# FFN norms in a diffusion backbone: 1/rms multiplied on behind the gate and up products, the shift as two extra columns

## The chip, the cores and the metric

One core of one Trainium2 chip runs the whole program. The metric is the device time of one execution in microseconds, as the median of several runs. The engines are TensorE (PE; its weight loads are shown as PEld), VectorE (DVE), ScalarE (ACT), GpSimd (POOL) and SyncE (SP), which issues most DMAs. They are tied together by semaphores only, and each works through its own instructions in the order written.

## The reference

Four layers. Each has a half-step SwiGLU FFN, a token mixer and a second half-step FFN, on 128 context tokens (xp) and 256 latent tokens (xs) of width 1024. Each sub-layer begins with an RMSNorm with adaLN modulation. The mixers are, in turn, gated DeltaNet, differential attention, a pooling mixer, and gated DeltaNet again. A final RMSNorm ends it.

```python
def _rms(x, g):
    y = xf * lax.rsqrt(jnp.mean(xf * xf, axis=-1, keepdims=True) + EPS) * g
def _adanorm(x, g, shift, scale):
    return _rms(x, g) * (1.0 + scale) + shift
def _half_ffn(x, m, j0, g, wg, wu, wd):
    h = _adanorm(x, g, m[:, :, j0], m[:, :, j0 + 1])
    f = (jax.nn.silu(h @ wg) * (h @ wu)) @ wd
    return x + 0.5 * m[:, :, j0 + 2] * f
...
for i in range(DEPTH):
    mp = _modulation(c_ctx[None, :], w_mod[i], b_mod[i])   # silu(c) @ w + b, 9 vectors of 1024
    ms = _modulation(c, w_mod[i], b_mod[i])
    xp = _half_ffn(xp, mp, 0, ...); xs = _half_ffn(xs, ms, 0, ...)
    # mixer on _adanorm(x, ..., 3, 4), with gate 5
    xp = _half_ffn(xp, mp, 6, ...); xs = _half_ffn(xs, ms, 6, ...)
```

Shift, scale and gate are vectors over channels, one set for context and one for latent tokens. D_FF is 2816.

## The kernel before

The residual stream `x` lies in SBUF as three token tiles of 128 tokens by 1024 channels. The program is a row of 12 stages, `r` = 0 to 11; stage r is an FFN when r % 3 is 0 or 2 and a mixer when it is 1. So there are 8 FFNs (stages 0, 2, 3, 5, 6, 8, 9, 11), and the crossings into them are: one at the start, four from a mixer (2, 5, 8, 11), three from an FFN (3, 6, 9). Four stages are entered as mixers from an FFN (1, 4, 7, 10).

Every product with weights is made of three float32r products. A value is rounded to its high part (`xT_hi`, `split_hi`, `hid_hi`, by ACT) and the difference is its low part (`xT_lo`, `split_lo`, `hid_lo`, by DVE); PE then adds hi x hi, hi x lo and lo x hi (`three`, line 1605).

**An FFN** works in 22 units. Unit j holds 128 columns of the gate weights, 128 of the up weights and 128 rows of the down weights: three parts of 128 x 1024, loaded by SP into two slots of `raw`. PE runs for each unit a gate pass (8 channel tiles x 3 matmuls of 384 token columns into bank 6), an up pass (the same into bank 7), and then the down pass of the unit before (3 token tiles x 2 halves x 3 matmuls of 512 columns into banks 0 to 5, which add up over the 22 units). ACT: rounds parts 0 and 1 of the next unit (line 778), takes silu of the gate bank (846), rounds the hidden tile (850), rounds part 2 of the next unit. DVE: `rest_part` 0 and 1 (the low parts, 1112), `hidden` = silu x up bank (1197), `hid_lo` (1199), `rest_part` 2, and then in the units that carry it the modulation work for the next layer, four `mod_junk` operations (398), each a product with a sum over a row of 1024. In FFNs 0 to 6 the 18 units of the middle bodies carry it (in FFN 0 also the first and the last two). SP loads the modulation weights and the raw parts in one order, and a modulation load waits for the DVE work before it.

**A crossing.** The residual (1225, 1228 on DVE, 622 on POOL): for each of three token tiles DVE multiplies two halves of the down banks by the gate (`gate_bc`) into three buffers `res_tmp`, POOL adds the first half to `x` and DVE the second. Then the norm: ACT squares a token tile with its row sum (809), POOL makes 1/rms (611, 612, a power of -0.5), DVE multiplies the tile by it into `xhat` (1158), PE transposes 24 blocks (1629), ACT applies scale and shift while it copies from PSUM (825, into four rows of `scratch`), and DVE casts to `xT_hi` (1172) and subtracts to `xT_lo` (1173). Each of the 8 channel tiles lets the first gate pass of the stage go on by three matmuls. In between PE makes the gate rows (1615): 4 matmuls of 512 columns that spread the gate vector of the stage over all partitions, which ACT copies to `gate_bc` (802). `diag`, their input, is made by DVE in the last body of the stage before (`gates`). In stage 0 the gate rows come behind the first up pass.

**Stage 0** begins with the modulation vectors themselves: five units on PE (2037), seven on DVE, all waiting for 1 MB loads; `normalised_rows(0)` stands in that work on DVE.

The order on each engine is written by hand; no scheduler moves anything.

## Time and profile before

| | us |
|---|---|
| median of 3 runs | 3479.87 |
| lowest, highest | 3478.95, 3481.42 |
| the profiled execution | 3476.7 |
| its span | 3474.9 |

The mean granted TensorE clock over the span is 0.973 of full. PE matmul is busy for 95% of the span, DVE for 68%, ACT for 38%, POOL for 9%. Busy time of PE is modelled, so its pace is better read from the starts of matmuls in the timeline. In the timeline a row has its start in us, its length in us, the engine, the line, the operation, out<-in, and in brackets how long the engine had been idle and what released it. Rows of the same kind that follow each other are merged (x4).

### The profile page before, as it was taken

To read this page: it belongs to the slowest core of one execution; us is meant where nothing else is said; L and a number is where in the kernel's file an instruction comes from. 1 tells how busy PE (TensorE), PEld (TensorE's weight loads), DVE (VectorE), ACT (ScalarE), POOL (GpSimd) and SP (SyncE) were. 2 spreads that over 40 slices of the span, in tenths; PEclk is the share of its full clock that TensorE was granted. 3 is DMA by queue.
4 is the path that set the end of the run, shared out by engine and by line. 5 is a ranking of instruction groups with operands and counts; after the bars stand their busy time and mean duration, and the time that the engine had idled before them with its cause. 6 is when DMAs were issued, how large, how long until landed. Compare 5 with 4: busy or idle time off the path is not lost.

```text
span 3474.9 us, 49765 instructions
## 1 busy us (share of the span) xinstructions
PE 3284.8 (95%) x18156; PEld 3051.1 (88%) x18156; DVE 2361.9 (68%) x3692; ACT 1310.5 (38%) x2253; POOL 297.2 (9%) x347
## 2 busy tenths in 40 slices
PE   7899999989999999879999998799999999999998
PEld 7799898979998998858998997699899988997997
DVE  7677876666776775566776777777767786666333
ACT  2233565243334334354334333333333366533332
POOL 0000104520000001000000001000000010540000
PEclk9999999999999999999999999899999999999999
DMA  6555220034544553213553553255345431013331
GB/s 261 208 211 211 101 81 1 25 134 181 211 183 162 208 202 121 85 49 140 211 214 131 200 206 153 79 211 211 146 192 205 189 107 57 14 49 109 127 127 73
DMA packets 62770, 502.77 MB, mean 145 GB/s; under 512 B 6416, under 2 KB 14608, under 8 KB 16448
## 3 DMA queue, kind: packets, MB, share of 16 engines
q1 hardware_dynamic: 60512, 493.12, 36.9%
q0 software_dynamic: 2144, 8.11, 0.6%
q8 instruction: 73, 1.20, 0.1%
q14 instruction: 41, 0.34, 0.0%
HBM read 496.49 MB, written 4.72 MB: 144 GB/s over the span
## 4 chain that ended last, share of the span: by engine, by line
PE 84%; DVE 9%; ACT 2%; issue 2%; DMA 1%; POOL 1%; SPq 0%; DVEq 0%; ACTq 0%; POOLq 0%
PE bank L1605 74%; PE bank L1768 7%; DVE xT_lo L1173 1%; DVE res_tmp L1225 1%; PE bank L1793 1%; DVE mod_junk L398 1%; DVE x L1228 1%; DMA mod_first<-mod_w 1%; DVE xT_hi L1172 1%; DVE split_lo L1112 1%; POOL rstd L612 1%; PE bank L1861 1%; PE bank L1719 1%; ACT split_hi L778 0%; DVE at_small L1489 0%
## 5 line engine op out<-in xcount | busy, mean ns | idle before, releaser
L1605 PE MATMUL bank<-xT_hi,split_hi 128*128 128x384 f32 (+1 forms) x3344 | 1142.5, 342 | 20.0 <-ACT silu_g L846 16.2
L1605 PE MATMUL bank<-xT_lo,split_hi 128*128 128x384 f32 (+1 forms) x3344 | 1132.3, 339 | 0.0
L1605 PE MATMUL bank<-xT_hi,split_lo 128*128 128x384 f32 (+1 forms) x3344 | 1131.6, 338 | 0.0
L1112 DVE TENSOR_TENSOR split_lo<-raw,split_hi 128x1024 fp32r<-128x1024 f32 x644 | 765.3, 1219 | 457.9 <-ACT split_hi L778 457.7
L778 ACT ACTIVATE split_hi<-raw 128x1024 fp32r<-128x1024 f32 x644 | 653.0, 1053 | 671.8 <-DMA raw<-ffn_w 367.8
L398 DVE SCALAR_TENSOR_TENSOR mod_junk<-mod_raw,cond 128x1024 f32<-128x1024 f32 x536 | 655.8, 1224 | 59.7 <-DVE mod_junk L398 33.3
L1605 PEld LDWEIGHTS bank<-xT_hi,split_hi 128*128 128x128 f32 (+1 forms) x3344 | 629.0, 188 | 43.0 <-DVE split_lo L1112 17.0
L1605 PEld LDWEIGHTS bank<-xT_lo,split_hi 128*128 128x128 f32 (+1 forms) x3344 | 629.0, 188 | 8.8 <-issue 0.4
L1605 PEld LDWEIGHTS bank<-xT_hi,split_lo 128*128 128x128 f32 (+1 forms) x3344 | 628.6, 188 | 1.1
L1605 PE MATMUL bank<-split_lo,hid_hi 128*128 128x512 f32 x1056 | 411.0, 389 | 0.0
L1605 PE MATMUL bank<-split_hi,hid_hi 128*128 128x512 f32 x1056 | 411.0, 389 | 0.0
L1605 PE MATMUL bank<-split_hi,hid_lo 128*128 128x512 f32 x1056 | 411.0, 389 | 0.0
L850 ACT ACTIVATE hid_hi<-hidden 128x384 fp32r<-128x384 f32 x176 | 92.4, 525 | 783.5 <-DVE hidden L1197 783.5
L622 POOL TENSOR_TENSOR x<-x,res_tmp 128x512 f32<-128x512 f32 x36 | 45.9, 1275 | 2479.2 <-DVE res_tmp L1225 2479.2
L1605 PEld LDWEIGHTS bank<-split_hi,hid_lo 128*128 128x128 f32 x1056 | 198.2, 188 | 41.1
L1605 PEld LDWEIGHTS bank<-split_hi,hid_hi 128*128 128x128 f32 x1056 | 198.1, 188 | 34.8
L1605 PEld LDWEIGHTS bank<-split_lo,hid_hi 128*128 128x128 f32 x1056 | 198.2, 188 | 34.7
L1197 DVE TENSOR_TENSOR hidden<-silu_g,bank 128x384 f32<-128x384 f32 x176 | 96.7, 549 | 162.2 <-PE bank L1605 162.2
L1199 DVE TENSOR_TENSOR hid_lo<-hidden,hid_hi 128x384 fp32r<-128x384 f32 x176 | 98.3, 558 | 109.0 <-ACT hid_hi L850 109.0
L1605 PE MATMUL bank<-split_hi,xT_hi 128*128 128x384 f32 (+2 forms) x360 | 136.4, 379 | 35.4 <-DVE xT_lo L1534 21.4
L1243 DVE SCALAR_TENSOR_TENSOR scratch<-scratch,cols 128x193 f32<-128x193 f32 x384 | 131.1, 415 | 12.0 <-ACT scratch L877 11.7
L1605 PE MATMUL bank<-split_lo,xT_hi 128*128 128x384 f32 (+2 forms) x360 | 133.2, 370 | 0.0
(247 smaller groups left out, 3068.2 us busy)
## 6 DMA issues: line engine op xcount, KB each, us to landing
raw<-ffn_w SPq DMA_DIRECT2D x176, 1536.0 KB, 7.6
mod_raw<-mod_w SPq DMA_DIRECT2D x134, 1024.0 KB, 4.8
raw<-a_in_w SPq DMA_DIRECT2D x20, 1536.0 KB, 6.3
raw<-b_in_w SPq DMA_DIRECT2D x8, 1536.0 KB, 6.3
raw<-a_out_w SPq DMA_DIRECT2D x4, 1536.0 KB, 7.7
mod_first<-mod_w SPq DMA_DIRECT2D x5, 1024.0 KB, 21.5
mod_first<-mod_rows SPq DMA_DIRECT2D x5, 1024.0 KB, 23.5
raw<-b_out_w SPq DMA_DIRECT2D x2, 1536.0 KB, 6.8
```

Of the source, the lines that this page charges most:

```text
L398: eng.scalar_tensor_tensor(mod_junk[:], weights[:, t], 1.0, cond[:, c], ALU.mult, ALU.mult, accum_out=mod_column(layer, unit, t, c)).then_ ...
L612: pool.tensor_tensor(rstd[:, span], rstd[:, span], neg_half[:, span], ALU.pow).then_inc(ready, 1)
L622: pool.tensor_tensor(x[:, t, 0:512], x[:, t, 0:512], res_tmp[:, 2 * t % 3], ALU.add).then_inc(res_pool, 1)
L778: act.activation(split_hi[:, unit.slot, q, 0:w], raw[:, unit.slot, q, 0:w], ACT.Copy).then_inc(hi_ready, 1)
L850: act.activation(hid_hi[:, par], hidden[:, par], ACT.Copy).then_inc(hid_hi_done, 1)
L1112: dve.tensor_tensor(split_lo[:, unit.slot, q, 0:w], raw[:, unit.slot, q, 0:w], f32(split_hi[:, unit.slot, q, 0:w]), ALU.subtract).then_inc ...
L1172: steps.settle(dve.tensor_copy(xT_hi[:, k], row))
L1197: dve.tensor_tensor(hidden[:, par], silu_g[:, par], ps[BANK_UP][:, 0:T], ALU.mult).then_inc(prod_done, 1)
L1199: dve.tensor_tensor(hid_lo[:, par], hidden[:, par], f32(hid_hi[:, par]), ALU.subtract).then_inc(hid_done, 1)
L1243: dve.scalar_tensor_tensor(dst, src, weight, dst, ALU.mult, ALU.add).then_inc(conv_step, 1)
L1605: ins = pe.matmul(out, lhsT, rhs, start=start and i == 0, stop=stop and i == 2)
L1768: ins = pe.matmul(ps[bank][:, h * P:(h + 1) * P], lhsT(h), rhs(h), start=True, stop=True)
```

## The change

In the FFN stages the norm is put together otherwise. Since 1/rms belongs to a token, and tokens are the columns of the gate and up products, it can be applied behind them:

- PE transposes `x` as it is. ACT rounds x times scale from PSUM into `xS_hi`, DVE forms the difference straight from PSUM into `xS_lo` (first the 128 context columns of all 8 tiles, then the 256 latent columns). `scratch`, `xhat` and the casts drop out.
- The shift vectors (context, latent) become columns 384 and 385 of `xS_hi` and `xS_lo`, so the gate and up matmuls have 386 columns.
- 1/rms is turned into three diagonal tiles (`rstd_diag`, DVE), spread over all partitions by one matmul of 384 columns behind the first up pass (`rstd_rows`), and copied by ACT to `rstd_bc`; its two last columns are 1.
- In each unit DVE multiplies the gate bank by `rstd_bc` into `gate_n`, and the up bank into `up_n`. ACT's silu takes the shift column as its bias, in two pieces (context, latent). DVE forms (up + shift column) x silu, again in two pieces.
- PE waits for `gate_norm` where it waited for silu, and for `up_norm` where it waited for the product.
- The gate rows of every FFN stage stand behind the first up pass and the rstd matmul. ACT copies them behind the first rounded hidden tile.
- The squares of token tiles 1 and 2 follow the rounding of the latent columns on ACT.
- `rest_part(..., 2)` of the first unit of a stage that follows an FFN moves from the last body of that FFN to behind the norm.

The mixer norms keep their form. The residual is regrouped in all stages: DVE makes all six products first, into `xhat`; POOL adds both halves of token tiles 0 and 1, DVE both of tile 2; POOL's three roots come behind its adds.

```diff
+    xS_hi = place("xS_hi", [P, KT, TC], F32R)
+    xT_hi, xT_lo = xS_hi[:, :, 0:T], xS_lo[:, :, 0:T]
...
+    def added(r, t):
+        return (res_pool, 4 * r + 2 * t + 2) if t < NT - 1 else (res_dve, 2 * r + 2)
...
         def residual(r):
-            for t in range(NT):
-                pool.wait_ge(res_prod, 6 * r + 2 * t + 1)
-                pool.tensor_tensor(x[:, t, 0:512], x[:, t, 0:512], res_tmp[:, 2 * t % 3], ALU.add).then_inc(res_pool, 1)
-                if t:
-                    norm_root(r + 1, t - 1)
-            norm_root(r + 1, NT - 1)
+            for t in range(NT - 1):
+                for half in range(2):
+                    pool.wait_ge(res_prod, 6 * r + 2 * t + half + 1)
+                    pool.tensor_tensor(x[:, t, span], x[:, t, span], xhat[:, t, span], ALU.add).then_inc(res_pool, 1)
+            for t in range(NT):
+                norm_root(r + 1, t)
...
+        def ffn_norm(r, f):
+            if r:
+                square(r, 0)
+            act.wait_ge(scale_ready, r + 1)
+            for c, (lo, hi) in enumerate(CHANNEL_SPANS):
+                for k in range(KT):
...
+                    ins = act.activation(xT_hi[:, k, lo:hi], turned(k, c), ACT.Copy, scale=scale_col[:, k, c:c + 1])
...
+            if r:
+                square(r, 1)
+                square(r, 2)
...
-                    act.wait_ge(part_done[0], done(unit, 0))
+                    if first and u == 0:
+                        act.wait_ge(rstd_mm, f + 1)
+                        act.activation(rstd_bc[:, 0:T], ps[BANK_RSTD][:, 0:T], ACT.Copy).then_inc(rstd_copied, 1)
+                    act.wait_ge(gate_norm, s0 + j + 1)
...
-                    act.activation(silu_g[:, par], ps[BANK_GATE][:, 0:T], ACT.Silu).then_inc(silu_done, 1)
+                    for c, (lo, hi) in enumerate(CHANNEL_SPANS):
+                        ins = act.activation(silu_g[:, par, lo:hi], gate_n[:, par, lo:hi], ACT.Silu, bias=gate_n[:, par, T + c:T + c + 1])
+                    ins.then_inc(silu_done, 1)
...
+        def ffn_norm(r, f):
+            dve.tensor_copy(xS_hi[:, :, T:TC], shift).then_inc(shift_hi, 1)
+            dve.tensor_copy(rstd_bc[:, T:TC], ones[:, 0:2]).then_inc(bc_ones, 1)
+            dve.wait_ge(shift_hi, f + 1)
+            dve.tensor_tensor(xS_lo[:, :, T:TC], shift, f32(xS_hi[:, :, T:TC]), ALU.subtract)
...
+                    ins = dve.scalar_tensor_tensor(xT_lo[:, k, lo:hi], turned(k, c), scale_col[:, k, c:c + 1],
+                                                   f32(xT_hi[:, k, lo:hi]), ALU.mult, ALU.subtract)
...
+            if r == 0 or by_stage[r - 1][0].name == "ffn":
+                rest_part(unit, 2)
+            for t in range(NT):
+                dve.wait_ge(rstd_ready, NT * r + t + 1)
+                dve.tensor_scalar(rstd_diag[:, t], ident[:], rstd[:, t:t + 1], None, ALU.mult).then_inc(rdiag_ready, 1)
...
+                    dve.wait_ge(part_done[0], done(unit, 0))
+                    dve.tensor_tensor(gate_n[:, par], ps[BANK_GATE][:, 0:TC], rstd_bc[:], ALU.mult).then_inc(gate_norm, 1)
+                    if nxt:
                         rest_part(nxt, 1)
                     dve.wait_ge(part_done[1], done(unit, 1))
+                    dve.tensor_tensor(up_n[:, par], ps[BANK_UP][:, 0:TC], rstd_bc[:], ALU.mult).then_inc(up_norm, 1)
+                    dve.wait_ge(up_norm, s0 + j + 1)
                     dve.wait_ge(silu_done, s0 + j + 1)
-                    dve.tensor_tensor(hidden[:, par], silu_g[:, par], ps[BANK_UP][:, 0:T], ALU.mult).then_inc(prod_done, 1)
+                    for c, (lo, hi) in enumerate(CHANNEL_SPANS):
+                        ins = dve.scalar_tensor_tensor(hidden[:, par, lo:hi], up_n[:, par, lo:hi], up_n[:, par, T + c:T + c + 1],
+                                                       silu_g[:, par, lo:hi], ALU.add, ALU.mult)
+                    ins.then_inc(prod_done, 1)
...
-                    if nxt:
+                    if nxt and not (last and u == 1):
                         rest_part(nxt, 2)
...
+        def rstd_rows(f):
+            pe.wait_ge(rdiag_ready, NT * (f + 1))
+            pe.matmul(ps[BANK_RSTD][:, 0:T], ones[:], rstd_diag[:].rearrange("p t c -> p (t c)"), start=True, stop=True).then_inc(rstd_mm, 1)
...
-                        pe.wait_ge(silu_done, s0 + j)
+                        pe.wait_ge(gate_norm, s0 + j)
...
-                            pe.wait_ge(prod_done, s0 + j)
+                            pe.wait_ge(up_norm, s0 + j)
...
                     if first and u == 0:
-                        if f == 0:
-                            gate_rows(0)
-                            pe.wait_ge(gate_ready, 4)
+                        rstd_rows(f)
+                        gate_rows(r)
                         continue
+                    if first:
+                        pe.wait_ge(rstd_copied, f + 1)
+                        pe.wait_ge(gate_ready, 4 * r + 4)
```

DVE, first unit of the loop over the middle units of an FFN, before (`split_lo` is `rest_part`):

```order
L1112 TENSOR_TENSOR split_lo<-raw,split_hi 128x1024
L1111 REGISTER_ALU
L1112 TENSOR_TENSOR split_lo<-raw,split_hi 128x1024
L1197 TENSOR_TENSOR hidden<-silu_g,bank 128x384
L1199 TENSOR_TENSOR hid_lo<-hidden,hid_hi 128x384
L1111 REGISTER_ALU
L1112 TENSOR_TENSOR split_lo<-raw,split_hi 128x1024
```

and the same place in the change:

```order
L1162 TENSOR_TENSOR split_lo<-raw,split_hi 128x1024
L1273 TENSOR_TENSOR gate_n<-bank,rstd_bc 128x386
L1161 REGISTER_ALU
L1162 TENSOR_TENSOR split_lo<-raw,split_hi 128x1024
L1277 TENSOR_TENSOR up_n<-bank,rstd_bc 128x386
L1281 SCALAR_TENSOR_TENSOR hidden<-up_n,silu_g 128x128
L1281 SCALAR_TENSOR_TENSOR hidden<-up_n,silu_g 128x256
L1285 TENSOR_TENSOR hid_lo<-hidden,hid_hi 128x384
L1161 REGISTER_ALU
L1162 TENSOR_TENSOR split_lo<-raw,split_hi 128x1024
```

Two multiplies stand between the splits, and the product is in two pieces.

DVE, the crossing from the second FFN (stage 2) to the third (stage 3), before:

```order
L1199 TENSOR_TENSOR hid_lo<-hidden,hid_hi 128x384
L1112 TENSOR_TENSOR split_lo<-raw,split_hi 128x1024
L1225 TENSOR_TENSOR res_tmp<-bank,gate_bc 128x512 x2
L1228 TENSOR_TENSOR x<-x,res_tmp 128x512
L1225 TENSOR_TENSOR res_tmp<-bank,gate_bc 128x512 x2
L1228 TENSOR_TENSOR x<-x,res_tmp 128x512
L1225 TENSOR_TENSOR res_tmp<-bank,gate_bc 128x512 x2
L1228 TENSOR_TENSOR x<-x,res_tmp 128x512
L1151 TENSOR_SCALAR scale_col<-modv 128x16
L1153 TENSOR_TENSOR scale_col<-scale_col,cols 128x16
L1158 TENSOR_SCALAR xhat<-x,rstd 128x1024 x3
L1172 CAST xT_hi<-scratch 128x384
```

and in the change:

```order
L1285 TENSOR_TENSOR hid_lo<-hidden,hid_hi 128x384
L1305 TENSOR_TENSOR xhat<-bank,gate_bc 128x512 x6
L1309 TENSOR_TENSOR x<-x,xhat 128x512 x2
L1201 TENSOR_SCALAR scale_col<-modv 128x16
L1203 TENSOR_TENSOR scale_col<-scale_col,cols 128x16
L1216 CAST xS_hi<-modv 128x8x2
L1217 COPY rstd_bc<-ones 128x2
L1219 TENSOR_TENSOR xS_lo<-modv,xS_hi 128x8x2
L1230 SCALAR_TENSOR_TENSOR xS_lo<-bank,scale_col,xS_hi 128x128 x8
L1230 SCALAR_TENSOR_TENSOR xS_lo<-bank,scale_col,xS_hi 128x256 x8
L1162 TENSOR_TENSOR split_lo<-raw,split_hi 128x1024
L1238 TENSOR_SCALAR rstd_diag<-ident,rstd 128x128 x3
```

The split_lo that stood ahead of the residual stands behind the differences.

PE, the same crossing, before (L1615 is the gate rows, L1629 the transposes):

```order
L1605 MATMUL bank<-split_hi,hid_lo 128x512
L1615 MATMUL bank<-diag,ones 128x512 x4
L1629 MATMUL bank<-ident,xhat 128x128 x24
L1605 MATMUL bank<-xT_hi,split_hi 128x384
L1605 MATMUL bank<-xT_lo,split_hi 128x384
```

and in the change the end of the first up pass of stage 3, where the gate rows are now:

```order
L1686 MATMUL bank<-xS_hi,split_hi 128x386
L1686 MATMUL bank<-xS_lo,split_hi 128x386
L1686 MATMUL bank<-xS_hi,split_lo 128x386
L1717 MATMUL bank<-rstd_diag,ones 128x384
L1696 MATMUL bank<-diag,ones 128x512 x4
L1686 MATMUL bank<-xS_hi,split_hi 128x386
```

The gate rows moved from behind the last down pass to behind the first up pass, 48 gate and up matmuls and 24 transposes later.

## Rows read from the trace of the kernel before

**Rows 1.** The page's part 4: chain of work that ended last, shares by engine.
```profile
PE 84%; DVE 9%; ACT 2%; issue 2%; DMA 1%; POOL 1%; SPq 0%; DVEq 0%; ACTq 0%; POOLq 0%
```

**Rows 2.** Timeline in mid-FFN, PE: start us, us, engine, line, operation, count.
```profile
130.63 0.34 PE L1605 MATMUL bank<-xT_hi,split_hi 128*128 128x384 f32 x1
...
139.11 0.39 PE L1605 MATMUL bank<-split_hi,hid_hi 128*128 128x512 f32 x1
...
143.19 0.34 PE L1605 MATMUL bank<-xT_hi,split_hi 128*128 128x384 f32 x1
```

**Rows 3.** Timeline in stage 0, DVE and ACT; brackets: idle before, releaser.
```profile
96.93 0.53 ACT L850 ACTIVATE hid_hi<-hidden 128x384 fp32r<-128x384 f32 x1 [1.57 <-DVE hidden L1197]
...
98.43 1.22 DVE L1112 TENSOR_TENSOR split_lo<-raw,split_hi 128x1024 fp32r<-128x1024 f32 x1 [0.39 <-ACT split_hi L778]
...
131.92 1.23 DVE L1112 TENSOR_TENSOR split_lo<-raw,split_hi 128x1024 fp32r<-128x1024 f32 x1 [2.64 <-ACT split_hi L778]
...
133.06 1.22 DVE L398 SCALAR_TENSOR_TENSOR mod_junk<-mod_raw,cond 128x1024 f32<-128x1024 f32 x1
...
138.37 2.35 DVE L1112 TENSOR_TENSOR split_lo<-raw,split_hi 128x1024 fp32r<-128x1024 f32 x2
...
140.65 0.55 DVE L1197 TENSOR_TENSOR hidden<-silu_g,bank 128x384 f32<-128x384 f32 x1
```

**Rows 4.** Groups by form: count, busy us, mean ns, idle before.
```profile
L1197 DVE TENSOR_TENSOR hidden<-silu_g,bank 128x384 f32<-128x384 f32 x176 | 96.7, 549 | 162.2 <-PE bank L1605 162.2
...
L990 ACT ACTIVATE att<-bank,dn_small 128x128 f32<-128x128 f32 x64 | 16.9, 414 | 29.8 <-PE bank L1768 29.8
...
L1397 DVE SCALAR_TENSOR_TENSOR wk<-bank,dn_small,att 128x128 f32<-128x128 f32 x64 | 16.9, 343 | 0.8 <-PE bank L1768 0.8
...
L1502 DVE SCALAR_TENSOR_TENSOR prob<-prob,at_small 128x384 f32<-128x384 f32 x16 | 9.9, 618 | 0.6
...
L1502 DVE SCALAR_TENSOR_TENSOR prob<-prob,at_small 128x128 f32<-128x128 f32 x8 | 2.8, 351 | 0.3
```

**Rows 5.** Timeline of the crossing from the second FFN to the third.
```profile
1037.77 1.23 DVE L1112 TENSOR_TENSOR split_lo<-raw,split_hi 128x1024 fp32r<-128x1024 f32 x1 [3.47 <-ACT split_hi L778]
...
1038.91 1.28 DVE L1225 TENSOR_TENSOR res_tmp<-bank,gate_bc 128x512 f32<-128x512 f32 x2
...
1039.67 1.29 POOL L622 TENSOR_TENSOR x<-x,res_tmp 128x512 f32<-128x512 f32 x1 [281.09 <-DVE res_tmp L1225]
...
1040.22 1.29 DVE L1228 TENSOR_TENSOR x<-x,res_tmp 128x512 f32<-128x512 f32 x1
...
1040.55 3.60 PE L1615 MATMUL bank<-diag,ones 128*128 128x512 f32 x8
...
1046.60 1.06 ACT L809 ACTIVATE xhat<-x 128x1024 f32<-128x1024 f32 x1 [1.35 <-DVE x L1228]
...
1063.18 0.34 PE L1605 MATMUL bank<-xT_hi,split_hi 128*128 128x384 f32 x1
```

**Rows 6.** The chain in order of time (start us, us, what): four passes of 384 columns.
```profile
491.30 1.29 PE bank L1719 x4
```

**Rows 7.** Timeline and chain in stage 0: DVE, DMA, PE.
```profile
73.19 1.23 DVE L1112 TENSOR_TENSOR split_lo<-raw,split_hi 128x1024 fp32r<-128x1024 f32 x1 [2.59 <-ACT split_hi L778]
...
105.40 7.91 DMA raw<-ffn_w
...
115.94 0.68 PE L1605 MATMUL bank<-xT_hi,split_hi 128*128 128x384 f32 x1 [5.64 <-ACT silu_g L846]
```

**Rows 8.** Windows (the number behind POOL's is the granted clock), and PE's timeline.
```profile
1049.00:1050.00 1.00, 0.19 (x2) 0.18 (x2) 0.75 (x1) 0.70 (x2) 0.00 (x0) 0.50 0.00 0
...
762.00:763.00 1.00, 1.00 (x9) 1.00 (x8) 0.97 (x3) 1.00 (x4) 0.00 (x0) 0.88 0.00 0
...
759.42 3.33 PE L1629 MATMUL bank<-ident,xhat 128*128 128x128 f32 x16 [0.81 <-DVE xhat L1158]
...
762.50 0.42 PE L1605 MATMUL bank<-xT_hi,split_hi 128*128 128x384 f32 x1
```

More of the change, by code:

```diff
@@ L32 @@
 T = TP + TS
+TC = T + 2
 NT = T // P
@@ L850, in body @@
                     act.activation(hid_hi[:, par], hidden[:, par], ACT.Copy).then_inc(hid_hi_done, 1)
-                    if first and u == 0 and f == 0:
-                        gate_rows(0)
+                    if first and u == 0:
+                        gate_rows(r)
                     if nxt:
@@ L1086, in _ @@
             kind = phs[0].name[0]
-            norm(r, to_pad=kind == "c")
             if kind == "f":
-                ffn(phs[0])
+                ffn_norm(r, phs[0].index)
+                ffn(phs[0], r)
+            else:
+                norm(r, to_pad=kind == "c")
             if kind == "a":
@@ L1574, in _ @@
             scales(r)
-            norm(r, to_pad=kind == "c")
             if kind == "f":
+                ffn_norm(r, phs[0].index)
                 ffn(phs[0], r)
+            else:
+                norm(r, to_pad=kind == "c")
             if kind == "a":
```

139 lines of the change are left out of this document (91 added, 48 removed).

## The prediction, made before the change was run

> **What bounds the kernel now.** I read four views, in this order. The chain of work that ended last says which engine to argue about: 84% of the span is TensorE (PE), 9% VectorE (DVE) [rows 1]. The timeline of one unit in the middle of an FFN gives PE's pace: the gate and up passes of a unit, 48 matmuls of 384 columns, run from 130.63 to 139.11, so 176.7 ns each, and the down pass, 18 matmuls of 512 columns, from there to 143.19, so 226.7 ns each [rows 2]. A unit takes 12.56 us, and 176 units fill most of the time. The same stretch on DVE and ScalarE (ACT) shows how much room the helpers have [rows 3]. The timeline of one crossing between two FFNs shows what PE waits for where it does wait [rows 5]; such crossings lie before each of the 12 sub-layers and at the end.
>
> **Two more columns.** All gate and up matmuls go from 384 to 386 columns: 8 FFNs x 22 units x 48 = 8448 matmuls. From [rows 2] 128 columns cost 50.0 ns, so 2 cost 0.78 ns, and 8448 of them **+6.6 us**, all on the path, since PE is back to back there. No row has a width that is no multiple of 128. The floor is 0 (the columns vanish in the fixed 27 ns that 384 columns leave over their slope), the ceiling is the 512-column row: +50 ns each, 420 us; I take the slope, which is what a stream of columns should show, and keep 0 as the near bound.
> The Trainium skill, page "TensorE: Matmul & The Clock Gate", section "Back-to-back issue gap", gives a sustained stream of weight load and matmul as about 81 ns at 128 columns and 131 ns at 512. By that slope (an estimate from the page) the two columns would cost 2.2 us in all; the trace's 226.7 ns at 512 columns disagrees with the page's level, so the trace is used.
>
> **A unit on DVE.** Added per unit: the gate multiply (386 columns from PSUM, as the product of 549 ns in [rows 4], about 0.47 us from start to start), the up multiply with a wait for its own end (0.59), and the product as two pieces of 128 and 256 columns. The form with a column operand takes 351 ns at 128 and 618 at 384 [rows 4], so 256 is about 485; with 80 ns overlap the two take 0.76 instead of 0.55. Together +1.27 us. Does it hide? In the 126 units that carry modulation work (18 in each of 7 FFNs) the DVE has a closed loop. Its pieces in [rows 3]: split_lo to first mod_junk 1.14, the four mod_junk 5.31, two split_lo 1.14 each, and from hid_hi's start to the next split_lo (98.43 - 96.93) 1.50 through ACT. With the new pieces: 1.14 + 5.31 + 1.14 + 0.47 + 1.14 + 0.59 + 0.78 + 1.50 = 12.07 us. PE's new unit is 12.60. So PE still sets the pace, with 0.5 us to spare; before, the spare is the wait for ACT of 2.64 at 131.92, of which 0.5 was the loop through ACT. I cost it at nothing; the cover is 0.5 us a unit, and without it see the rival. PE's own waits move to earlier events (gate_norm instead of silu_done, up_norm instead of prod_done), with over 3 us of room in a normal unit. In the last body the work for the next gates stands ahead on DVE, and I count about 0.4 us left.
>
> **The residual.** Call R the start of the first product. Now it is 1038.91, held up by the split_lo of 1037.77; PE had finished the first token tile 12 matmuls before 1040.55, that is at 1038.05. The change moves this split_lo behind the norm, so R comes 0.86 earlier where an FFN ends and another weight phase with a third part follows. The six products at 0.64 end at R+3.85. GpSimd (POOL) now has four adds of 1.29 from R+0.76, DVE two. The two engines hinder each other: POOL's add runs 1039.67 to 1040.96, and DVE's, started at 1040.22, ends at 1041.51, 0.55 after POOL's [rows 5]; and all its 36 adds look so. So DVE's adds need 0.55 each but queue with POOL's: the last ends at R+0.76+5.16+1.10 = **R+7.0** (R+7.6 now). If DVE had the port first it would be R+5.2; POOL is on its third add by then, so I take 7.0.
>
> **Into an FFN (7 times, stage 0 apart).** From D, the end of the adds: scale_ready D+0.4. ACT rounds 8 tiles of 128 columns from PSUM (414 ns, 0.265 spacing [rows 4]) and DVE's differences follow by fours (343 ns, 0.264 spacing): done D+3.8. The first 256-column difference ends at D+4.3 and PE starts at D+4.35; ACT and DVE then give a tile every 0.40, PE wants one every 0.53, so PE is no longer fed slowly. Two passes 8.5, to D+12.85. The squares of tiles 1 and 2, their roots and the three rstd_diag are ready at about D+9.5, hidden behind these passes. Then on PE: the rstd broadcast, half of 1.29 [rows 6] = 0.65, and the gate rows, 3.60 [rows 5]. **The gate rows lay at 1040.55 in the shadow of the residual and now lie in the stream.** Unit 1 starts at D+17.1; its wait for the gate multiply (1.2 after the broadcast) hides behind the gate rows. From an FFN: 1038.05+7.0+17.1 = 1062.15 against 1063.18 now: -1.0, three times. From a mixer R does not move (its splits end before it), so the 0.86 is missing: about -0.2, four times. Together **-3.8 us**. Bounds per entry: -1.8 (POOL keeps the port, DVE's adds overlap) to +2.2 (clock, below).
>
> **Into a mixer, and the end.** The third square now starts 7.7 after R (1046.60 [rows 5]). In the new order it follows the second, which waits for POOL's fourth add (R+5.9, or 6.45 if a DVE add slips in): R+7.15 to R+7.7. So it gains 0.86 from R at two mixers, nothing from R at the pooling mixer and at the end, loses 0.4 at the first mixer (there DVE is late by the unit work above), and 0 to 0.55 everywhere, taken as 0.25: **-2.6 us**. The moved split_lo (1.14) hides in the 1.6 us that DVE waits for ACT's first tile; one row shorter and it would show.
>
> **Stage 0.** The three xhat products leave the start (three of about 0.7 us), but DVE then waits for the last weights; no row says when these land, so the start gains between 0 and 2.1, taken as 0.8. Then the chain is DVE, SyncE, DMA: burst of mod_junk, load of the next weights (7.91), split, PE [rows 7]. Up to the first burst the path now holds the broadcast, its copy, and the multiplies: I get 74.5 against 73.19 [rows 7]. The second turn has one unit more of DVE work (+1.3), and PE then waits for gate_n behind split_lo and not for silu_g: +0.3. PE's steady start moves from 115.94 to 118.8: **+2.9 us**.
>
> **Sum.** +6.6 - 3.8 - 2.6 + 2.9 = +3.1 us. The profiled execution took 3476.7 (span 3474.9); its changed form would take 3479.8. It lies 3.2 under the median of the runs, so on the median's scale: **3483 us**, +0.1%. About 0.2% (7 us) is what a measurement of this kernel can tell from no change.
>
> **The rivals.**
> *DVE becomes the bound (the slower side).* If the loop above exceeds 12.60, each of the 18 units in a row adds the excess; PE starts to wait once 3.1 us have piled up (its gate wait). It decides from 0.7 us above my 12.07. At 12.9: 18 x 0.3 - 3.1 = 2.3 us, seven times, 16 us: 3499. For: three forms here have no row of their own, and register work sits between them. Against: each piece that has a row fits. 13%.
> *The clock is low in the gate pass.* Now the granted clock falls to half at about 1049.0 [rows 8], after PE had ended its gate rows at 1044.15 [rows 5] and then paused over 3 us. Afterwards PE has transposes at R+3.3 to 5.2 and R+6 to 10, and the first product at R+11.35. If it runs at 1.2 GHz for some 5 us, a tile costs 0.96 instead of 0.53 (three matmuls at twice the time for their columns): +2.2 an entry, 15 us in all: 3498. Against: at about 762.2 the clock was back before the first product at 762.50, when PE had done nothing but transposes since 759.42 [rows 8], so transposes keep it up, and the gaps between them are 1 us. The Trainium skill, page "TensorE: Matmul & The Clock Gate", section "Part 4: PE-mode transpose", says that transposes don't count as work for the clock gate; by that rule the clock would fall at all seven entries, which is this rival; the trace at 762.2 disagrees with it. 12%.
> *The columns are free and the port is kind.* Without the 6.6 us, and with the adds 0.55 sooner at 12 crossings: 3470 to 3473. For: the spacing of 384 columns holds a fixed part of 27 ns that could hide them. Against: the slope between the two widths. 18%.
> *The width is padded.* If 386 runs as 400, +52 us: 3535. Nothing but the missing row speaks for it. 4%.
> The forecast keeps 53%, with about 6 us to either side for the entries and stage 0.
>
> **How the numbers follow.** The range goes from 3468 (columns free, port kind, entries well) to 3500 (either of the two slower cases); outside are the padded width, a loop above 12.9 and some of the faster tail, under 2 in 10. Faster by over 0.2% (below 3473): nearly the third case: 17%. Slower (above 3487): 13 + 12 + 4, and a little of the forecast's tail, some of it overlapping: 31%. Same: 52%.
>
> **What the changed profile would show.** Spacing of gate matmuls 177.5 ns (units 12.60); a wait of 0.4 to 0.6 us of DVE's split_lo for ACT in mod units, not zero; PE idle in mid-FFN nil; the DVE adds at the residual about 1.3 us each with the last ending at R+7.0; a PE row of 3.6 us of gate rows after the first up pass; granted clock 1.0 in the first gate pass; first unbroken unit at about 118.8. The prediction is wrong if PE waits for DVE in mid-FFN, if the clock is half in the gate passes, or if the spacing isn't 0.8 ns wider.

## The result, and the profile after

| | before | after |
|---|---|---|
| median, us | 3479.8 | 3501.03 |
| lowest, highest | 3478.95, 3481.42 | 3500.88, 3501.68 |
| the profiled execution | 3476.7 | 3501.68 |
| its span | 3474.9 | 3499.9 |

The changed kernel is slower: ratio 1.0065, 95% interval 1.0053 to 1.0077. The forecast was 3483 with 3500 as the upper end. Between the profiled executions lie 25.0 us, between the medians 21.2; the ledger below goes by the spans.

The page of the changed kernel, part 4, and the group of part 5 that holds the gate and up matmuls (mean ns of one, then idle time and releaser):

```profile
PE 86%; DVE 7%; ACT 2%; POOL 2%; DMA 1%; issue 1%; SPq 0%; DVEq 0%; POOLq 0%; ACTq 0%
...
L1686 PE MATMUL bank<-xS_hi,split_hi 128*128 128x386 f32 (+2 forms) x3344 | 1150.8, 344 | 38.4 <-DVE gate_n L1273 20.4
```

Against [rows 1] PE's share of the path has gone up, DVE's down: the norms did leave the path, and more than their time came back on PE.

One unit in mid-FFN of the changed kernel, PE's timeline (start, us, engine, line, operation): down pass, gate and up passes, next down pass.

```profile
131.14 0.40 PE L1686 MATMUL bank<-split_hi,hid_hi 128*128 128x512 f32 x1
...
135.27 0.34 PE L1686 MATMUL bank<-xS_hi,split_hi 128*128 128x386 f32 x1
...
143.78 0.40 PE L1686 MATMUL bank<-split_hi,hid_hi 128*128 128x512 f32 x1
```

Gate and up take 8.51 (8.52 in the median unit), against 8.48 in [rows 2], as forecast. But **the down pass takes 4.13 instead of 4.08**, and nothing in it was changed: the same 18 matmuls of 512 columns, the same order. The first twelve start 0.231 us apart on average, the last six 0.227 as before. 0.05 us by 176 units is 8.8 us.

The mixers show the same. The projections of the first DeltaNet have 384 columns in both kernels; two starts that lie 48 matmuls apart, before:

```profile
400.31 0.34 PE L1605 MATMUL bank<-xT_hi,split_hi 128*128 128x384 f32 x1
...
408.63 0.34 PE L1605 MATMUL bank<-xT_hi,split_hi 128*128 128x384 f32 x1
```

and after:

```profile
405.09 0.34 PE L1686 MATMUL bank<-xS_hi,split_hi 128*128 128x384 f32 x1
...
413.54 0.34 PE L1686 MATMUL bank<-xS_hi,split_hi 128*128 128x384 f32 x1
```

8.32 us became 8.45; over runs of 579 matmuls the mean goes from 173.5 to 176.3 ns. This row of before also says something that the prediction missed: 384 columns ran at 173.5 ns in the mixer and at 176.7 in the FFN [rows 2] of the same kernel.

Even one FFN of the kernel before shows both paces. In stage 3, unit 1 goes from 1063.18 [rows 5] to its down pass at 1071.50, so 8.32 us for 48 matmuls, 173.3 ns each; then come the first down pass and unit 2:

```profile
1071.50 0.40 PE L1605 MATMUL bank<-split_hi,hid_hi 128*128 128x512 f32 x1
1075.62 0.34 PE L1605 MATMUL bank<-xT_hi,split_hi 128*128 128x384 f32 x1
...
1084.10 0.39 PE L1605 MATMUL bank<-split_hi,hid_hi 128*128 128x512 f32 x1
```

Unit 2 takes 8.48 us, and so does every unit behind it, also those that read the same slot as unit 1. So at these addresses either pace can occur, and what ran before has a say; behind the first down pass of an FFN the slow one stays.

A crossing into an FFN (stage 3) in the changed kernel, DVE, POOL and PE:

```profile
1047.44 2.58 DVE L1305 TENSOR_TENSOR xhat<-bank,gate_bc 128x512 f32<-128x512 f32 x4 [3.07 <-PE bank L1686]
...
1048.21 5.43 POOL L647 TENSOR_TENSOR x<-x,xhat 128x512 f32<-128x512 f32 x4 [277.99 <-DVE xhat L1305]
...
1051.39 2.80 DVE L1309 TENSOR_TENSOR x<-x,xhat 128x512 f32<-128x512 f32 x2
...
1058.40 0.41 PE L1686 MATMUL bank<-xS_hi,split_hi 128*128 128x386 f32 x1 [2.73 <-DVE xS_lo L1230]
...
1068.53 0.81 PE L1717 MATMUL bank<-rstd_diag,ones 128*128 128x384 f32 x2
1069.18 3.60 PE L1696 MATMUL bank<-diag,ones 128*128 128x512 f32 x8
...
1072.21 0.74 PE L1686 MATMUL bank<-xS_hi,split_hi 128*128 128x386 f32 x1
1072.79 0.34 PE L1686 MATMUL bank<-xS_lo,split_hi 128*128 128x386 f32 x1
```

With R = 1047.44 the adds end at R+6.75, the first matmul starts at R+10.96, and unit 1 starts at R+24.8, its second matmul not before R+25.35 (0.58 after the first; modelled starts run into the gate rows there). The two passes took 10.1 instead of 8.5, because ten matmuls started 0.32 apart. The windows of these stretches (the number behind POOL's is the granted clock):

```profile
1060.00:1061.00 1.00, 1.00 (x4) 1.00 (x4) 1.00 (x4) 1.00 (x3) 0.19 (x1) 0.50 0.00 0
1062.00:1063.00 1.00, 1.00 (x5) 1.00 (x5) 0.61 (x3) 1.00 (x2) 0.83 (x3) 0.50 0.00 0
1064.00:1065.00 1.00, 1.00 (x8) 1.00 (x7) 0.99 (x1) 0.00 (x0) 0.00 (x0) 1.00 0.73 258
...
2518.00:2519.00 1.00, 1.00 (x7) 1.00 (x6) 0.60 (x6) 0.63 (x3) 0.67 (x2) 0.50 0.00 0
2521.00:2522.00 1.00, 0.00 (x0) 0.00 (x0) 1.00 (x4) 1.00 (x4) 0.00 (x0) 1.00 0.00 0
```

All seven entries have a low stretch. At stages 2, 3, 5 and 6 it lies in the first gate pass (1.55 us lost at each); at stages 8, 9 and 11 it lies ahead of it (at stage 9 from 2517.1 to 2520.6, first gate matmul at 2522.24), and those three have none of the slow matmuls.

### The profile page after: what moved, and what is told of

It reads as the page before. It is cut to its first block, busy times and chain, and to the rows that moved or that the text cites. A ratio compares the mean times of both kernels' runs of the same rounds, so it can differ in the third digit from the quotient of the medians.

```text
span 3499.9 us, 50480 instructions
## 1 busy us (share of the span) xinstructions
PE 3303.9 (94%) x18172; PEld 3067.1 (88%) x18172; DVE 2548.9 (73%) x4232; ACT 1368.6 (39%) x2437; POOL 313.6 (9%) x359
## 4 chain that ended last, share of the span: by engine, by line
PE 86%; DVE 7%; ACT 2%; POOL 2%; DMA 1%; issue 1%; SPq 0%; DVEq 0%; POOLq 0%; ACTq 0%
PE bank L1686 75%; PE bank L1869 7%; PE bank L1894 1%; DMA mod_raw<-mod_w 1%; POOL x L647 1%; DVE mod_junk L421 1%; PE bank L1696 1%; POOL rstd L635 1%; DVE split_lo L1162 1%; PE bank L1962 1%; DVE xS_lo L1230 1%; PE bank L1820 1%; DVE x L1309 1%; DVE xhat L1305 0%; DVE at_small L1570 0%
## 5 line engine op out<-in xcount | busy, mean ns | idle before, releaser
L1686 PE MATMUL bank<-xS_hi,split_hi 128*128 128x386 f32 (+2 forms) x3344 | 1150.8, 344 | 38.4 <-DVE gate_n L1273 20.4
L1686 PE MATMUL bank<-xS_lo,split_hi 128*128 128x386 f32 (+2 forms) x3344 | 1139.2, 341 | 0.0
L1686 PE MATMUL bank<-xS_hi,split_lo 128*128 128x386 f32 (+2 forms) x3344 | 1137.3, 340 | 0.0
L1686 PEld LDWEIGHTS bank<-xS_hi,split_hi 128*128 128x128 f32 (+1 forms) x3344 | 631.5, 189 | 55.2 <-issue 21.5
L1686 PEld LDWEIGHTS bank<-xS_lo,split_hi 128*128 128x128 f32 (+1 forms) x3344 | 635.7, 190 | 10.7 <-issue 2.3
L1686 PEld LDWEIGHTS bank<-xS_hi,split_lo 128*128 128x128 f32 (+1 forms) x3344 | 633.4, 189 | 1.1
L893 ACT ACTIVATE silu_g<-gate_n 128x128 f32<-128x128 f32 x352 | 141.6, 449 | 581.6 <-DVE gate_n L1273 581.6
L647 POOL TENSOR_TENSOR x<-x,xhat 128x512 f32<-128x512 f32 x48 | 65.1, 1383 | 2437.6 <-DVE xhat L1305 2437.6
L1686 PE MATMUL bank<-split_hi,xS_hi 128*128 128x384 f32 (+2 forms) x360 | 138.7, 385 | 33.9 <-DVE xS_lo L1615 19.6
L1277 DVE TENSOR_TENSOR up_n<-bank,rstd_bc 128x386 f32<-128x386 f32 x176 | 97.8, 556 | 83.2 <-PE bank L1686 83.2
## 6 DMA issues: line engine op xcount, KB each, us to landing
mod_first<-mod_w SPq DMA_DIRECT2D x5, 1024.0 KB, 21.9
```

What stands on the lines that cost most here:

```text
L647: pool.tensor_tensor(x[:, t, span], x[:, t, span], xhat[:, t, span], ALU.add).then_inc(res_pool, 1)
L893: ins = act.activation(silu_g[:, par, lo:hi], gate_n[:, par, lo:hi], ACT.Silu, bias=gate_n[:, par, T + c:T + c + 1])
L1277: dve.tensor_tensor(up_n[:, par], ps[BANK_UP][:, 0:TC], rstd_bc[:], ALU.mult).then_inc(up_norm, 1)
L1686: ins = pe.matmul(out, lhsT, rhs, start=start and i == 0, stop=stop and i == 2)
```

## The experiments

**1. What makes unchanged matmuls slower?** In the changed kernel the rows of xT, now xS, are 386 elements long, 1544 bytes; so xS_hi and xS_lo take 12352 bytes each instead of 12288, and all tiles behind them, split_hi, split_lo and the hidden tiles among them, lie 128 bytes further on in SBUF. (A matmul has a stationary operand, which is loaded as weights, and a moving one, whose columns stream past it. In gate and up passes the split tiles are stationary and xT moves; in the down pass the hidden tiles are stationary and the split tiles move.) Four kernels take this apart, b_pad:

```diff
     xT_lo = place("xT_lo", [P, KT, T], F32R)
+    place("pad", [P, 32])
```

> The kernel before with 128 bytes of nothing behind xT_lo, so that split_hi and split_lo lie 128 bytes further on in SBUF, as they do in the changed kernel; rows of xT stay 1536 bytes. Theory A (the changed kernel's slower TensorE streams come from rows of xT that are 1544 bytes long): no change, 3480, down pass 4.08 us. Theory B (it is where the split tiles lie): down pass 4.13 us, 3489 or more. Theory C (the two columns alone do it): no change.

b_stride:

```diff
+    xS_hi = place("xS_hi", [P, KT, T + 2], F32R)
+    xS_lo = place("xS_lo", [P, KT, T + 2], F32R)
+    xT_hi, xT_lo = xS_hi[:, :, 0:T], xS_lo[:, :, 0:T]
```

> The kernel before with rows of 386 elements (1544 bytes) in xT_hi and xT_lo, of which 384 are used, so nothing but addresses differs. Theory A (row length): the projections of the mixers go from 173.3 to 176.1 ns a matmul, the down pass from 4.08 to 4.13 us a unit (176 x 0.05 = 8.8 us), with the mixers some 14 us in all, 3494. Theory B (split tiles): the same, and b_pad too. Theory C (columns): no change, 3480.

b_cols, on top of b_stride:

```diff
+            if r % 3 != 1:
+                two = modv[:, 0, 0:KT]
+                dve.tensor_copy(xS_hi[:, :, T:T + 2], two)
+                dve.tensor_copy(xS_lo[:, :, T:T + 2], two)
...
-                            ins = three(ps[bank][:, 0:T], split_hi[:, unit.slot, q, w], split_lo[:, unit.slot, q, w],
-                                        xT_hi[:, kk], xT_lo[:, kk], kk == 0, kk == KT - 1)
+                            ins = three(ps[bank][:, 0:T + 2], split_hi[:, unit.slot, q, w], split_lo[:, unit.slot, q, w],
+                                        xS_hi[:, kk], xS_lo[:, kk], kk == 0, kk == KT - 1)
```

> The kernel before with 386 columns in all gate and up matmuls (the last two are filled with numbers nobody uses) and rows of 386 elements; norm, residual and DVE work per unit stay as before, save two small copies in each FFN norm (0.3 us, 7 times on the path, 2.4). Theory A: 14 us for the row length, 6.6 for the columns, 2.4 for the copies: 3503. Theory C: 0.09 us a unit for the columns, 15.6, and the copies: 3498.

a_392, the changed kernel with

```diff
-    xS_hi = place("xS_hi", [P, KT, TC], F32R)
-    xS_lo = place("xS_lo", [P, KT, TC], F32R)
+    xS_hi_w = place("xS_hi", [P, KT, 392], F32R)
+    xS_lo_w = place("xS_lo", [P, KT, 392], F32R)
+    xS_hi, xS_lo = xS_hi_w[:, :, 0:TC], xS_lo_w[:, :, 0:TC]
```

> The changed kernel with rows of 392 elements (1568 bytes, a multiple of 32) in xS, 386 of them used; the matmuls stay 386 columns wide. Theory A, if what hurts is that 1544 bytes is no multiple of 32: down pass back to 4.08 us, projections of the mixers at 173.3 ns, so 8.8 + 6 us less than the changed kernel, 3486. Theory C: the same as the changed kernel, 3501.

| kernel | median | ratio to before, 95% | gate + up | down | mixer, ns |
|---|---|---|---|---|---|
| before | 3478.7 | | 8.48 | 4.08 | 173.5 |
| b_pad | 3455.59 | 0.9934 (0.9918 to 0.9951) | 8.32 | 4.09 | 173.5 |
| b_stride | 3482.8 | 1.0011 (1.0001 to 1.0020) | 8.46 | 4.10 | 176.3 |
| b_cols | 3500.04 | 1.0061 (1.0045 to 1.0078) | 8.52 | 4.13 | 176.3 |
| a_392 | 3487.76 | 1.0027 (1.0017 to 1.0038) | 8.48 | 4.10 | 175.4 |
| after | 3501.03 | 1.0065 (1.0053 to 1.0077) | 8.52 | 4.13 | 176.3 |

No theory had foreseen b_pad: **128 unused bytes make the kernel 23 us faster**. Its unit late in the last FFN:

```profile
3204.32 0.39 PE L1606 MATMUL bank<-split_hi,hid_hi 128*128 128x512 f32 x1
...
3208.41 0.34 PE L1606 MATMUL bank<-xT_hi,split_hi 128*128 128x384 f32 x1
...
3216.73 0.39 PE L1606 MATMUL bank<-split_hi,hid_hi 128*128 128x512 f32 x1
```

8.32 us for the 48 matmuls, 173.3 ns each, the pace that the mixers had all along, and here no unit of the middle bodies runs slower. So the kernel before itself lost 0.16 us a unit. Theory A fell as it was put: b_stride moved the FFN units by nothing in sum, and costs 4.1 us, about the mixers' 2 x 792 matmuls by 2.8 ns (4.4). Theory C was not far for b_cols (3498), but its down pass moved too. a_392 came out near theory A's 3486, but not by its terms: the down pass went back to 4.10, the mixers only to 175.4, and the gate and up passes, of which nothing was expected, gave 0.04 us a unit. And b_cols alone, with none of the new norm, reaches 3500.04, of which its own copies are 2.4 by the estimate above.

**2. TensorE by itself.**

> A kernel that leaves out everything but TensorE: in 23 blocks it streams the matmuls of two FFN units (48 gate and up, 18 down), four times over, on tiles of zeros, and in each block the tiles stand at other addresses or have other row lengths. Blocks 1 and 2 are the addresses of the kernel before and of the one with 128 bytes of pad, block 15 the long rows of 1544 bytes, block 16 the same with 386 columns. If TensorE's own reads of its two operands collide by their addresses, blocks 1, 2, 15 and 16 repeat what the whole kernels show: 8.48, 8.32, 8.46 and 8.52 us for the gate and up matmuls, 4.08, 4.09, 4.10 and 4.13 us for the down matmuls, and the other blocks tell which distances are good. If the slow streams need the other engines' traffic in SBUF, all blocks with 384 columns run at 8.32 and 4.08 us, and those with 386 at 8.36.

Each block is cut out by marker matmuls of 64 columns. Blocks 3 and 4, gate and up matmuls only, at the addresses of before and 128 bytes further:

```profile
259.31 0.28 PE L186 MATMUL bank<-buf 128*128 128x64 f32 x1
...
327.34 0.19 PE L206 MATMUL bank<-buf 128*128 128x64 f32 x1
327.37 0.27 PE L186 MATMUL bank<-buf 128*128 128x64 f32 x1
...
394.12 0.19 PE L206 MATMUL bank<-buf 128*128 128x64 f32 x1
```

8 units in 68.0 and in 66.75 us, less 0.11 for the marker: 8.49 and 8.33 a unit. Whole units (gate, up, down), with split and hidden tiles shifted:

| shift, bytes | 0 | 32 | 64 | 128 | 192 | 256 | 320 | 384 | 448 | 512 |
|---|---|---|---|---|---|---|---|---|---|---|
| us a unit | 12.56* | 12.48 | 12.54 | 12.42 | 12.48 | 12.56 | 12.53 | 12.42 | 12.48 | 12.56 |

(* block 1 holds the start of the clock and measures nothing here, so the whole kernel's value stands there; block 3 measures its gate and up part, 8.49.) Rows of 1544 bytes with 384 columns gave 12.57, with 386 columns 12.66. The three that were measured (12.42, 12.57, 12.66) match the whole kernels (12.41, 12.56, 12.65), and the shift of 256 bytes matches the kernel before (12.56). So the slow pace needs no other engine: **the same matmuls on PE alone run at different paces by where their operands lie**, and the pattern returns with 256 bytes. Shifting the split tiles alone gave 12.54, the hidden tiles alone 12.58; it takes both to reach 12.42.

> TensorE alone again. Gate and up matmuls of 384, 386, 388, 392, 400 and 416 columns, rows all 2048 bytes apart, with the stationary tiles moved in steps of 32 bytes over 256; then down matmuls with the same steps. In the first bench a shift of 128 bytes took the unit from 12.56 to 12.42 us, and a shift of 256 brought it back. If the cost is one of phase between the two operands (theory A), 386 columns have a good place too: 8.36 us for 48 matmuls (174.2 ns each) at one of the eight, 8.5 at others. If a width that is no multiple of some number of columns costs by itself, 386 stays at 8.5 us or above in all eight, and 400 or 416 reach their floor of 180.0 and 186.7 ns.

> TensorE alone: 386 columns in layouts that fit the changed kernel, rows of 386, 388 and 392 elements, the low tile 0, 64, 128 or 192 bytes off a multiple of 256 from the high one, the stationary tiles in steps of 32 bytes. Theory A: with rows that are no multiple of 256 bytes apart the distance runs through good and bad places from row to row, so all of them lie between 8.36 and 8.55 us, none at 8.36; the changed kernel's own layout gives 8.52.

48 matmuls with rows 2048 bytes apart, over the eight shifts, against the width divided by 2.4 columns a ns plus 13.3 ns:

| columns | 384 | 386 | 388 | 392 | 400 | 416 |
|---|---|---|---|---|---|---|
| by the formula | 8.32 | 8.36 | 8.40 | 8.48 | 8.64 | 8.96 |
| best of eight | 8.335 | 8.415 | 8.49 | 8.44 | 8.655 | 8.975 |
| worst of eight | 8.49 | 8.65 | 8.65 | 8.65 | 8.97 | 9.29 |
| at the best within 0.01 | 5 | 1 | 5 | 1 | 3 | 3 |

384 columns are within 0.02 us of the formula at five shifts of eight, 386 at none, though one comes within 0.06 (and 392 beats it by 0.04 at one, so it is no strict floor). In bench3, with layouts that fit, 96 places of 386 columns lie between 8.42 and 8.59 us; the layout of the changed kernel gives 8.54. The best, 8.42, is what one gets with xS_lo and all behind it 320 bytes further on.

**3. Does this hold in the whole kernel?**

```diff
+    place("pad", [P, 80])
     xS_lo = place("xS_lo", [P, KT, TC], F32R)
```

> The changed kernel with 320 bytes of nothing between xS_hi and xS_lo; rows and widths as they are. TensorE alone ran 48 matmuls of 386 columns in 8.54 us at the changed kernel's distances and in 8.42 us at these. Theory A (TensorE's pace hangs on the distance between its two operands' addresses, whatever the other engines do): gate and up matmuls 8.40 to 8.42 us instead of 8.52, down pass 4.08 to 4.13, so 18 to 30 us less, about 3476. Rival (in the whole kernel the phase is set by waits and by what came before): no change, 3501.

Measured: 3470.72, ratio 0.9984 (0.9974 to 0.9993); gate and up 8.40, down 4.08, so 0.17 us a unit. In this group of runs the kernel before took 3476.62 and not 3479.8, so gains on the changed kernel go by the ratios: 1.0065 - 0.9984 is 28 us. 0.17 us by 176 units make 30. The rival (no change) is out. A unit of the last FFN:

```profile
3200.40 0.39 PE L1687 MATMUL bank<-split_hi,hid_hi 128*128 128x512 f32 x1
...
3204.48 0.33 PE L1687 MATMUL bank<-xS_hi,split_hi 128*128 128x386 f32 x1
...
3212.88 0.39 PE L1687 MATMUL bank<-split_hi,hid_hi 128*128 128x512 f32 x1
```

And the counter-test, b_pad with 64 instead of 32 elements:

> The kernel before with 256 bytes of nothing behind xT_lo instead of 128. Theory A (only the distance of the two operands modulo 256 bytes counts): the pad of 256 undoes what the pad of 128 gave, gate and up matmuls at 8.48 us and down pass at 4.08, 3479. Rival (any pad helps, by moving other tiles, or the 128-byte kernel was a lucky build): 3456, as with 128.

Measured: 3478.66 beside 3478.89, ratio 1.0001 (0.9991 to 1.0010); its unit is back at 8.48 and 4.08:

```profile
3203.20 0.34 PE L1606 MATMUL bank<-xT_hi,split_hi 128*128 128x384 f32 x1
...
3211.68 0.39 PE L1606 MATMUL bank<-split_hi,hid_hi 128*128 128x512 f32 x1
...
3215.76 0.34 PE L1606 MATMUL bank<-xT_hi,split_hi 128*128 128x384 f32 x1
```

The rival of a lucky build is out. But theory A, that only the distance modulo 256 bytes counts, holds for these pads and not in general: the bench has the kernel before's distances modulo 256 with rows 1536 and 2048 bytes apart, and 48 matmuls take 8.49 us with the one and 8.335 with the other.

**4. The gate rows.** On the changed kernel:

```diff
         def ffn_norm(r, f):
             if r:
                 square(r, 0)
+                act.wait_ge(res_prod, 6 * r)
+                gate_rows(r)
...
                 pe.wait_ge(x_in, 16 * NT)
+            else:
+                gate_rows(r)
...
                         rstd_rows(f)
-                        gate_rows(r)
+                        if r == 0:
+                            gate_rows(r)
```

> The changed kernel with the gate rows of stages 2, 3, 5, 6, 8, 9 and 11 back where they were, on TensorE ahead of the transposes of the norm (their copies on ScalarE behind the first square). Theory 1 (3.6 us of gate rows lie in the stream at each of the seven entries, and were hidden before): unit 1 starts 3.0 to 3.6 us sooner, 21 to 25 us in all, about 3478. Theory 2 (the gate rows only fill a wait that would be there without them, for the gate multiply): under 1.5 us an entry, 3491 or more. Where the clock's low stretch moves with them, 1.5 us more or less at an entry.

Measured: 3486.52, ratio 1.0028 (1.0016 to 1.0039), so by the ratios 13 us less than the changed kernel, 1.8 an entry, between the two theories. PE at stage 3 says why:

```profile
1066.76 0.81 PE L1721 MATMUL bank<-rstd_diag,ones 128*128 128x384 f32 x2
1068.74 0.44 PE L1688 MATMUL bank<-xS_hi,split_hi 128*128 128x386 f32 x1 [1.17 <-DVE gate_n L1275]
```

Without the 3.6 us of gate rows PE waits 1.2 us for the gate multiply, which they had covered. 0.65 for the broadcast and 1.33 more lie between the two rows, 1.98 in all; with the gate rows it was 0.65 and 3.4, so 2.1 more.

Both together:

> Both edits together, the 320 bytes and the gate rows. They touch different stretches, so they should add up: 3501 - 25 - 23 = 3453.

Measured: 3457.70, ratio 0.9946 (0.9930 to 0.9963). By the ratios 1.0065 - 0.0081 - 0.0037 = 0.9947: they add up; the gate rows gave 13 us and not 23. This is the changed kernel at its best place found, and it stands beside b_pad, the kernel before at its own (0.9934, 0.9918 to 0.9951). So once both are placed well, no gain of the new norm is left that these runs could show.

**5. The residual alone.** b_pad with the six products into xhat, four adds on POOL and two on DVE, the roots behind the adds, and the split_lo behind the norm's multiplies, as in the diff of the change.

> The kernel before with 128 bytes of pad (3455.6 so far) and of the change only the regrouped residual and the split_lo that is moved behind the norm. By the changed kernel's trace the adds end 6.75 instead of 7.6 us after the first product, the first product comes 0.8 us sooner where an FFN ends, and the norm's transposes 0.3 sooner: 1.1 us at six crossings, 0.4 at six: 9 us less, 3447. Rival (the moved split_lo, 1.2 us, delays the casts of the norm, since here DVE needs two operations a tile): no gain or a loss, 3455 to 3462.

Measured: 3451.43, ratio 0.9927 (0.9910 to 0.9944). Against b_pad's 0.9934 that is 2 us, inside the noise of either ratio, and not the forecast 9. The two profiled spans differ by 2.8 us (3453.4 and 3450.6), and 1.7 of them lie ahead of the first residual. So the regrouping is not shown to gain anything. DVE at the crossing into stage 3 (R = 1029.42):

```profile
1036.93 0.75 DVE L1162 TENSOR_SCALAR xhat<-x,rstd 128x1024 f32<-128x1024 f32 x1 [0.45 <-POOL rstd L616]
1038.40 0.75 DVE L1162 TENSOR_SCALAR xhat<-x,rstd 128x1024 f32<-128x1024 f32 x1 [0.72 <-POOL rstd L616]
1039.87 0.75 DVE L1162 TENSOR_SCALAR xhat<-x,rstd 128x1024 f32<-128x1024 f32 x1 [0.71 <-POOL rstd L616]
1040.53 1.22 DVE L1116 TENSOR_TENSOR split_lo<-raw,split_hi 128x1024 fp32r<-128x1024 f32 x1
1042.19 0.36 DVE L1178 CAST xT_hi<-scratch 128x384 fp32r<-128x384 f32 x1 [0.44 <-ACT scratch L829]
```

The adds end at R+6.75 instead of R+7.6, but the third multiply starts at R+10.45, where b_pad has it at R+10.09. Now the three roots stand behind POOL's adds and come every 1.47 us; with the old grouping POOL made the first two between and behind its adds, DVE multiplied two tiles in one go, and the third root waited for the third square. **POOL's queue took the place of the squares.** The moved split_lo is hidden: DVE waits another 0.44 for ACT behind it.

## Why the prediction was wrong, point by point

On the spans, forecast and measured:

| term | forecast | measured |
|---|---|---|
| gate and up matmuls | +6.6 | +6.6 (0.037 x 176) |
| down pass | none | +8.8 |
| DeltaNet projections | none | +4.4 (1584 x 2.8 ns) |
| into an FFN, seven times | -3.8 | -0.9 |
| stage 0 up to PE's steady start | +2.9 | +5.0 (120.99) |
| into mixers, end, clock inside the mixers | -2.6 | +1.1 (the rest) |
| sum | +3.1 | +25.0 |

**The step that failed is "Two more columns".** It took the slope between 384 and 512 columns of [rows 2] and put every other matmul at nothing, without a reason. Those others cost 13.2 of the 21.9 us that the sum missed; b_cols and b_stride, which have none of the new norm, show them. Its figure of 0.78 ns came true, and by accident. 384 columns in the FFN stood 3.3 ns above their floor, so the slope was too flat (0.39 ns a column where 0.417 fits the other rows) and the "fixed 27 ns" was 13.3 of fixed time, which the 512-column row shows as well (226.7 - 213.3), and the rest the slow pace of these addresses. Well placed kernels give another price: 8.32 us for 384 columns (b_pad) against 8.40 for 386 (a_pad), 1.7 ns a matmul, and no place tested for 386 columns reached the formula. What the step lacked was the side effect of the two columns: longer rows and a shift of 128 bytes, in which matmuls elsewhere lose 0.05 us a down pass and 2.8 ns each in the projections. Its bounds (0 to +50 ns a gate matmul) did not cover that, since they were bounds on the wrong instructions. The four rivals have no place for it either; the case "columns are free" was the near end of it. That 3501 lies close to the clock rival's 3498 and the DVE rival's 3499 is chance: the clock gave 6.2 of the 25 us, and the DVE loop nothing.
The Trainium skill, page "SBUF — State Buffer", section "SBUF: two separate sides", says that on the engine side only the port pair of VectorE and GpSimd contends and that TensorE, with a second read port for its weights, waits for nobody. That no other engine slows it agrees with bench1. Two reads that are free of each other would leave open why the same 48 matmuls take 8.33 and 8.49 us at two addresses. That it is these two reads that collide is a guess; no run here shows it.

**Into an FFN.** The steps hold to 0.4 us: R comes 0.81 earlier (0.86), the adds end at R+6.75 (7.0), PE starts 4.2 behind them (4.35), the gate rows cost 3.4 of stream (3.6), the gate multiply hides behind them. The three entries without a low clock in the gate pass gain 1.5 (stage 9) and 0.65 (8 and 11, from mixers), where 1.0 and 0.2 were forecast. In the other four the clock rival came true, at 1.55 an entry instead of 2.2, 6.2 us in all in the profiled execution, and with it one of the prediction's own signs of being wrong. I argued from 762.2 that transposes keep the clock up. In the changed kernel PE goes from the last transposes (1053.70 to 1055.67) through an idle 2.7 us to the first gate matmul, and the clock falls at 1059.7. At stage 9 it falls at 2517.1, while PE waits between the two groups of transposes:

```profile
2514.64 1.10 PE L1709 MATMUL bank<-ident,x 128*128 128x128 f32 x8 [0.73 <-POOL x L647]
2517.55 3.41 PE L1709 MATMUL bank<-ident,x 128*128 128x128 f32 x16 [1.81 <-POOL x L647]
```

The Trainium skill, page "TensorE: Matmul & The Clock Gate", section "Part 4: PE-mode transpose", has it that transposes don't count as work for the gate; by that the clock falls at all seven entries, and so it did. But by that it would not come back before the first gate matmul, and at stage 9 it was back at 2520.6, when PE had run nothing but transposes since 2514.64, as at 762.2 in the kernel before. So the reading of 762.2 was right and what I drew from it was wrong: the clock can come back in transposes and still fall in the waits beside them. In a_rows, where 3.6 us of ordinary matmuls run ahead of the transposes, stages 8, 9 and 11 have no low stretch at all; stages 2, 3, 5 and 6 keep theirs, in the same place. In a_pad, with the changed kernel's order, only stages 5 and 11 have it in the gate pass. What an entry gets was not settled.

**Into mixers and the end.** The adds came as forecast, and so did R, save at the first mixer (below). "So it gains 0 to 0.55 everywhere, taken as 0.25" failed: the third square does start 0.4 sooner, but the roots behind the adds are late next (third multiply at R+10.4 instead of R+10.1), so each mixer norm loses about 0.35. The final norm gains 0.44 (third multiply at R+13.2 instead of R+13.65). The split_lo hides, as said. The rest of this line of the table, some 3 us, lies inside the mixers, where the low stretches of the clock differ between the two executions; it was not taken apart.

**Stage 0.** Two estimates missed in the same direction: the start gained nothing (DVE is through with its modulation rows at 53.17, before at 53.09, since it waits for weights), and broadcast, copy and two multiplies sit one after another ahead of the first burst. It begins at 76.64, not at 74.5; PE's steady start moves by 5.0.

DVE's split_lo ahead of the first burst, and PE's two late unit starts in stage 0:

```profile
76.64 1.23 DVE L1162 TENSOR_TENSOR split_lo<-raw,split_hi 128x1024 fp32r<-128x1024 f32 x1 [2.34 <-ACT split_hi L802]
...
99.34 0.69 PE L1686 MATMUL bank<-xS_hi,split_hi 128*128 128x386 f32 x1 [13.61 <-DVE gate_n L1273]
...
120.99 0.69 PE L1686 MATMUL bank<-xS_hi,split_hi 128*128 128x386 f32 x1 [6.75 <-DVE gate_n L1273]
```

**What was right: DVE keeps its spare.** A modulation unit of the changed kernel:

```profile
161.85 1.23 DVE L1162 TENSOR_TENSOR split_lo<-raw,split_hi 128x1024 fp32r<-128x1024 f32 x1 [0.97 <-ACT split_hi L802]
...
168.31 1.22 DVE L1162 TENSOR_TENSOR split_lo<-raw,split_hi 128x1024 fp32r<-128x1024 f32 x1
169.45 0.56 DVE L1273 TENSOR_TENSOR gate_n<-bank,rstd_bc 128x386 f32<-128x386 f32 x1
...
171.05 0.56 DVE L1277 TENSOR_TENSOR up_n<-bank,rstd_bc 128x386 f32<-128x386 f32 x1
...
174.50 1.23 DVE L1162 TENSOR_TENSOR split_lo<-raw,split_hi 128x1024 fp32r<-128x1024 f32 x1 [0.96 <-ACT split_hi L802]
```

Of the 0.96 us of waiting 0.39 is the way through ACT, as in [rows 3], which leaves 0.57 spare; 0.5 was forecast. Once stage 0 runs steadily (from 120.99), PE never waits in the 18 middle units of an FFN, and the rival of the DVE loop is out.

One wait stands at the end of stage 0, where the last two units carry modulation work too. "I count about 0.4 us left" failed there, by 2.0 us; PE waits for the low part of the hidden tile:

```profile
365.07 0.50 PE L1686 MATMUL bank<-split_hi,hid_hi 128*128 128x512 f32 x1 [2.00 <-DVE hid_lo L1285]
```

It adds nothing to the time. DVE has four more mod_junk ahead of the residual in both kernels; the residual starts 5.8 us later than before (369.88 against 364.09), and the late start of the stage alone makes 5.0 of that, the slower units 1.7.

## What to carry to other kernels

When a change makes a tile longer, list every tile placed behind it and every matmul that reads one, and look whether the same shape of matmul already runs at two paces in the profile: if it does, a pad of 32 to 128 bytes is worth a run before any restructuring (here 128 bytes gave 23 us). Before work is moved off a queue in one step of a chain, ask who stands behind it in the same queue: the adds ended 0.85 us sooner, and the roots behind them made the third multiply 0.35 later. And what fills a wait (the gate rows over the gate multiply) is worth less to move than its own length, about 2 of 3.4 us here.
